# Search for the best pairs of the first two tiles divided into five parts at steps of their own; the first tile's search begins at step 36 instead of 40

## What is computed

```python
def peer_ffn(xn, w_query, sub_keys, u, v):
    def one_block(xb):                                   # 128 tokens
        q = (xb @ w_query).reshape(BLOCK, PEER_HEADS, 2, PEER_HALF)
        s = jnp.einsum('thcd,hckd->thck', q, sub_keys)   # scores against 2 x 128 sub-keys, 8 heads
        s1, i1 = lax.top_k(s[:, :, 0], PEER_TOPK)        # 16 best of each half
        s2, i2 = lax.top_k(s[:, :, 1], PEER_TOPK)
        cand_s = (s1[..., :, None] + s2[..., None, :]).reshape(BLOCK, PEER_HEADS, 256)
        cand_i = (i1[..., :, None] * N_KEYS + i2[..., None, :]).reshape(BLOCK, PEER_HEADS, 256)
        top_s, top_c = lax.top_k(cand_s, PEER_TOPK)      # 16 best pairs
        expert = jnp.take_along_axis(cand_i, top_c, axis=-1)
        g = jax.nn.softmax(top_s.astype(jnp.float32), axis=-1)
        ue, ve = jnp.take(u, expert, axis=0), jnp.take(v, expert, axis=0)
        act = jax.nn.gelu(jnp.einsum('thkd,td->thk', ue, xb), approximate=False)
        return jnp.einsum('thk,thkd->td', g * act, ve)
```

## Time and profile before

| what | value |
|---|---|
| median of 3 runs | 1881.32 us (1880.59 to 1883.3) |
| the profiled execution's own time | 1884.28 us |
| its span | 1882.5 us |
| mean granted TensorE clock | 0.967 |
| busy, share of the span | PE 94%, PEld 79%, DVE 71%, ACT 38%, POOL 35% |
| steps 36 to 62 in the span | about 490 to 735 us |

### The profile page before, as it was taken

How to read it: one execution, slowest core, us unless ns; L and a number is a source line. 1 busy time by engine, 2 the same in 40 slices (tenths; PEclk the granted TensorE clock), 3 DMA queues, 4 the chain that set the end, 5 groups by cost and what they waited for, 6 DMA issues and landing times.

```text
span 1882.5 us, 24827 instructions
## 1 busy us (share of the span) xinstructions
PE 1778.0 (94%) x8763; PEld 1483.5 (79%) x8767; DVE 1344.6 (71%) x2706; ACT 721.2 (38%) x1201; POOL 660.8 (35%) x416
## 2 busy tenths in 40 slices
PE   5899998999878989999989998999899999999998
PEld 4788875554555678999989998999788888888886
DVE  6843268465546877979979953992588888888886
ACT  4333334141222232355435533553343343343342
POOL 3234320000000332677676777776322222222220
PEclk9899997999898999999989999999899999999999
DMA  3222202434242662588887899886999999899993
GB/s 126 68 84 95 91 30 105 158 110 152 96 155 90 206 201 84 163 294 282 281 325 261 286 360 406 309 284 208 362 361 334 327 333 333 328 333 332 328 333 118
DMA packets 170192, 429.78 MB, mean 228 GB/s; under 512 B 15328, under 2 KB 66144, under 8 KB 165744
## 3 DMA queue, kind: packets, MB, share of 16 engines
q1 hardware_dynamic: 133056, 294.23, 45.4%
q0 software_dynamic: 36864, 134.23, 19.3%
q10 hardware_dynamic: 176, 0.07, 0.0%
HBM read 384.44 MB, written 44.04 MB: 228 GB/s over the span
## 4 chain that ended last, share of the span: by engine, by line
PE 73%; DVE 6%; DMA 3%; ACT 1%; issue 1%; POOL 1%; DVEq 0%; ACTq 0%
PE psum L1864 28%; PE psum L1161 8%; PE psum L1162 8%; PE psum L1163 8%; PE psum L1103 6%; PE psum L1187 5%; PE psum L1090 3%; PE psum L1011 3%; DMA u<-in_u 2%; PE psum L1059 1%; POOL ul L1401 1%; PE psum L1142 1%; DMA act_mat<-act_w 1%; DVE nmax L1460 1%; DVE hits L1615 1%
## 5 line engine op out<-in xcount | busy, mean ns | idle before, releaser
L1401 POOL TENSOR_TENSOR ul<-u,uh 128x1024 fp32r<-128x1024 f32 x128 | 321.8, 2515 | 532.3 <-ACT uh L1319 531.0
L1161 PE MATMUL psum<-split,uh 128*128 128x384 f32 x1024 | 357.0, 349 | 13.8 <-POOL ul L1401 13.8
L1163 PE MATMUL psum<-split,ul 128*128 128x384 f32 x1024 | 345.1, 337 | 0.0
L1162 PE MATMUL psum<-split,uh 128*128 128x384 f32 x1024 | 345.1, 337 | 0.0
L1844 POOL DMA_INDIRECT v_row<-in_v,gv x128 | 122.3, 956 | 383.5 <-DVE psum L1922 369.9
L1864 PE MATMUL psum<-vl,wh 128*128 128x512 f32 x768 | 240.9, 395 | 0.0
L1161 PEld LDWEIGHTS psum<-split,uh 128*128 128x128 f32 x1024 | 194.6, 190 | 18.0 <-POOL ul L1401 16.3
L1162 PEld LDWEIGHTS psum<-split,uh 128*128 128x128 f32 x1024 | 194.6, 190 | 1.4 <-issue 1.4
L1163 PEld LDWEIGHTS psum<-split,ul 128*128 128x128 f32 x1024 | 194.1, 190 | 0.0
L1864 PEld LDWEIGHTS psum<-vl,wh 128*128 128x128 f32 x768 | 144.9, 189 | 33.9
L1922 DVE SCALAR_TENSOR_TENSOR psum<-v_row,w,psum 128x1024 f32<-128x1024 f32 x127 | 162.8, 1282 | 0.0
(11 more groups left out here) (291 smaller groups left out, 3376.0 us busy)
## 6 DMA issues: line engine op xcount, KB each, us to landing
u<-in_u SPq DMA_DIRECT2D x128, 512.0 KB, 5.0
v<-in_v SPq DMA_DIRECT2D x64, 1024.0 KB, 5.0
act_mat<-act_w SPq DMA_DIRECT2D x128, 192.0 KB, 5.1
act_v<-act_mat SPq DMA_DIRECT2D x64, 384.0 KB, 6.7
wraw<-in_w_wide SPq DMA_DIRECT2D x18, 1024.0 KB, 5.1
gate_mat<-stage SPq DMA_DIRECT2D x16, 1024.0 KB, 10.1
gate<-gate_mat SPq DMA_DIRECT2D x128, 128.0 KB, 6.1
w_low<-in_w_branch_b SPq DMA_DIRECT2D x8, 1024.0 KB, 5.2
```

Of the source, the lines that this page charges most:

```text
L1161: nc.tensor.matmul(out, high[:, c], split[:, 0:DENSE, 0, c], start=(c == 0), stop=False)
L1162: nc.tensor.matmul(out, high[:, c], split[:, 0:DENSE, 1, c], start=False, stop=False)
L1163: last = nc.tensor.matmul(out, low[:, c], split[:, 0:DENSE, 0, c], start=False, stop=(c == DC - 1))
L1401: nc.gpsimd.tensor_tensor(ul[:, n % U_COLS], u[:, n % U_COLS], uh[:, n % UH_COLS].bitcast(F32), ALU.subtract).then_inc(s["u_low"], 1)
```

## The change

`best` is cut into its five parts, `best(part)`, the last with the cast and the shift. The tables now give each part a step. For search 0 the `find` parts move from steps 40 to 44 to steps 36 to 40, `pair_up` from 45 to 41, and `best` from step 46 to steps 42 to 46; its picks stay. For search 1 `find` and `pair_up` stay; `best` goes from step 58 to steps 58, 58, 59, 59 and 60, and the four picks from steps 59, 60, 61, 62 to 61, 61, 62, 62. ScalarE's `exps(0)` stays at step 47, and `exps(1)` goes from step 59 to step 61. No instruction is added or taken away.

```diff
-FIND_AT = ((40, 41, 42, 43, 44), (52, 53, 54, 55, 56))
-PAIR_AT = (45, 57)
-BEST_AT = (46, 58)
-PICK_AT = ((48, 49, 50, 51), (59, 60, 61, 62))
+FIND_AT = ((36, 37, 38, 39, 40), (52, 53, 54, 55, 56))
+PAIR_AT = (41, 57)
+BEST_AT = ((42, 43, 44, 45, 46), (58, 58, 59, 59, 60))
+PICK_AT = ((48, 49, 50, 51), (61, 61, 62, 62))
...
-                if step == BEST_AT[0] + 1:
+                if step == BEST_AT[0][-1] + 1:
                     exps(0)
...
-            def best():
-                for part in range(5):
-                    link(search(part, top, top_at, cand, PEER_HEADS))
+            def best(part):
+                link(search(part, top, top_at, cand, PEER_HEADS))
+                if part < 4:
+                    return
                 link(nc.vector.tensor_copy(top_at_f[:], top_at[:]))
...
-                    if step == BEST_AT[r]:
-                        best()
-                    if step in PICK_AT[r]:
-                        pick_out(HIT_HEADS * PICK_AT[r].index(step))
+                    for part in range(5):
+                        if step == BEST_AT[r][part]:
+                            best(part)
+                    for k, at in enumerate(PICK_AT[r]):
+                        if step == at:
+                            pick_out(HIT_HEADS * k)
```

More of the change, by code:

```diff
@@ L1371, in _ @@
                     column(step - 1 - FIRST_COLUMN)
-                if step == BEST_AT[1] + 1:
+                if step == BEST_AT[1][-1] + 1:
                     exps(1)
@@ L1664, in chosen_beside @@
                 for r in range(2):
-                    if step in FIND_AT[r]:
-                        find(r, FIND_AT[r].index(step))
+                    for part in range(5):
+                        if step == FIND_AT[r][part]:
+                            find(r, part)
                     if step == PAIR_AT[r]:
                         pair_up()
-                    if step == BEST_AT[r]:
-                        best()
-                    if step in PICK_AT[r]:
-                        pick_out(HIT_HEADS * PICK_AT[r].index(step))
+                    for part in range(5):
+                        if step == BEST_AT[r][part]:
+                            best(part)
+                    for k, at in enumerate(PICK_AT[r]):
+                        if step == at:
+                            pick_out(HIT_HEADS * k)
                     if step == SETTLE_AT[r]:
```

## The result

| what | before | changed |
|---|---|---|
| median of 6 runs each, the two side by side | 1880.95 us (1876.89 to 1883.74) | 1866.09 us (1857.45 to 1868.38) |
| ratio, 95% interval | 1 | 0.9908 (0.989 to 0.9925) |
| the profiled execution's own time | 1884.28 us | 1865.89 us |
| its span, mean granted TensorE clock | 1882.5 us, 0.967 | 1864.1 us, 0.974 |

The changed kernel is 0.9% faster by the ratio; the two medians lie 14.9 us (0.8%) apart, and the ratio is not their quotient. Between the two profiled executions lie 18.4 us, forecast 16.6.

The account below looks back on a forecast made before the run. TensorE, busy 94% of the span, was taken to wait mainly for VectorE, with low clock behind gaps. Terms −1.1 + 3.2 + 1.2 + 5.9 + 7.4 = 16.6 us gave 1867.7 us profiled, 1864.7 us median; range 1860.5 to 1871.

Parts of the forecast that it names:

- A: Steps 36 to 41: find parts placed earlier, one uncovered ahead of out_b, lose 1.1 us (bounds 0.9 to 2.1).
- B: Step 43: out_a comes earlier, its 2.18 us wait ends and value runs faster, a gain of 3.2 us.
- C: OUT_LEFT in step 43: starts from a busy stretch instead of a low clock, a gain of 1.2 us (0 to 3.0).
- D: Steps 46 to 51: refinement and row start earlier, fewer GpSimd holds, a gain of 5.9 us (1.8 to 6.4).
- E: Steps 58 to 60: waits for row and headT and the slow QUERY_LEFT go, gain 7.4 us (at least 5.8).
- the gap is shorter than any in rows 2 that had a low clock behind it: Steps 36 to 41: reason for taking a loss of 1.1 us, not 2.1 with value at low clock too.
- I take 1.2, near the second row: OUT_LEFT, step 43: chosen between 0 and 3.0 us, near the 1.4 from a similar product behind 3.60 us of idle.
- rival of the long gain: OUT_LEFT at full clock (+1.8) and no VectorE hold (+0.5): 18.9 us gained, 1862.4 us; chance 0.12.
- short gain: Bad VectorE holds, or OUT_LEFT and step 39's value at low clock: 1868.2 us, 1872 with nearly all; chance 0.18.
- a wait of 0.5 to 2 us for `out_b` in step 51: Step 51: sign that VectorE, with three picks ahead of out_b, sets the time; before, TensorE waited 0.16 us.
- rival of full DMA engines: Around 1130 us: DMA traffic ends independently of TensorE, so up to 16.6 us is returned, 1881 us; chance 0.07.
- rival that the clock turns the sign: Steps 36 to 45: added VectorE parts keep TensorE's clock at 0.50, three slow products cost 21 us, 1886 us; chance 0.03.

Follow-up runs that it names:

- three_parts_early: Changed kernel, search 0's find parts at steps 36, 37, 38, 42, 43, pair_up at 45, best whole at 46: 1875.53 us, ratio 0.996.
- same_again: The changed kernel unaltered, run once more: 1862.46 us, ratio 0.989 to the kernel before.
- search0_only: Changed kernel with search 1 put back at its old steps, so only search 0 is moved: 1873.17 us, ratio 0.9949.
- picks_only: Changed kernel with best of search 1 whole at step 58, its picks staying at 61, 61, 62, 62: 1867.14 us, ratio 0.9918.
- two_more_picks: Changed kernel with the last pick of search 1 made two more times in step 62: 1864.49 us, ratio 0.9907.
- four_more_picks: Changed kernel with the last pick of search 1 made four more times in step 62: 1875.44 us, ratio 0.9961.
- best_whole_at_46: Changed kernel with best of search 0 left whole at step 46: 1869.48 us, ratio 0.9932.
- search1_only: Changed kernel with search 0 put back at its old steps 40 to 46, so only search 1 is moved: 1873.99 us, ratio 0.9955.
- part_behind_out_b: Changed kernel with search 0's third find part moved behind out_b to step 39 and the fourth to 40: 1864.72 us, ratio 0.9891.
- part_behind_again: The kernel of part_behind_out_b run once more: 1860.96 us, ratio 0.9885.

## Why the prediction was right, and where its terms were not

| term | forecast | measured, changed kernel |
|---|---|---|
| A, steps 36 to 41 | -1.1 (-0.9 to -2.1) | -4.1 |
| B, `out_a` in step 43 | +3.2 | +3.4 |
| C, `OUT_LEFT` | +1.2 (0 to 3.0) | +2.9 |
| D, steps 46 to 51 | +5.9 (1.8 to 6.4) | +6.2 |
| E, steps 58 to 60 | +7.4 (5.8 or more) | +7.8 |
| sum | 16.6 | 16.2 |

**A was mis-sized, and outside its bounds.** The step "TensorE starts near 527.65 for 526.57" held: the wait is 0.99 us. What failed is the reason given for its clock, "the gap is shorter than any in rows 2 that had a low clock behind it". The gap was read alone; it lies between one of 2.17 us and one of 2.60, which were there before. The bound of 2.1 failed with it, since it allowed the low clock for `value` of step 39 only. In the changed kernel `value` of step 40 takes 1.89 us for 1.47 and `BRANCH_B` 8.83 for 7.13; with the slower turns of `out_b` and of the scores between them this makes the other 3 us. How often this happens, over the eight profiles in which the third part stands in front of `out_b` and the copies are as before:

| wait for out_b | profiles | 38 to 42 | BRANCH_B | OUT_LEFT |
|---|---|---|---|---|
| 0.92, 0.97, 0.99 | three_parts_early, same_again, changed | 42.6 to 42.7 | 8.83 | 8.83, 7.13, 7.13 |
| 0.67 to 0.90 | search0_only, picks_only, two_more_picks, four_more_picks, best_whole_at_46 | 39.4 to 39.8 | 7.13 | 7.13 |
| none | before, search1_only, part_behind_out_b, part_behind_again | 38.5 to 38.6 | 7.13 | 10.04 to 10.14 |

Five of eight came out near the forecast (0.9 to 1.3 us lost), three at 4.1. The order by the length of the wait is clean in these profiles, but the two groups are only 0.02 us apart. The length isn't the cause either: in all eight the wait ends 6.13 or 6.14 us after the turn of `row` in step 38 began, so VectorE's part is equally late, and only TensorE's arrival differs. It differs by where the low clock behind the gap of 2.17 us ended. The first four matmuls of the next scores, in the changed kernel and in search0_only:

```profile
524.20 1.67 PE L1011 MATMUL psum<-akT,abqT 128*128 128x512 f32 x4
```

```profile
523.83 2.15 PE L1011 MATMUL psum<-akT,abqT 128*128 128x512 f32 x4
```

In the four profiles with a wait of 0.67 or 0.68 us these four took 2.15 or 2.16 us, in the four with 0.90 to 0.99 they took 1.67 to 1.75; the second is also the picture in the four profiles without the wait (1.65 to 1.74), where `BRANCH_B` was never slow. So with the early return of the clock `BRANCH_B` was slow in three of four profiles with the wait and in none of four without it, and with the late return in none of four. What makes the clock return early or late in the same code, and why `BRANCH_B` was fast in best_whole_at_46 (wait of 0.90 us) and slow in three_parts_early (0.92), stays open.

**B** held to 0.2 us: the wait of 2.18 us is gone, and `value` takes 1.36 us for 2.35, as worked out.

**C** came out at its upper end: the step "I take 1.2, near the second row" priced `OUT_LEFT` from a product behind another gap. And its reason, that the engine comes from a busy stretch, is not the cause: that stretch is as busy in part_behind_out_b, where `OUT_LEFT` takes 10.05 us. C is coupled to A: without the wait in step 39 `OUT_LEFT` was slow, with it it was fast in seven of eight, and `BRANCH_B` was slow in three. What makes the one follow from the other is not shown. A and C taken as one sum to -1.2 here, +1.7 in the five profiles with the shorter wait, and 0 with the part behind `out_b`; the forecast had +0.1. The total came out right in part by luck: A was 3.0 us worse than forecast, C 1.7 better. The rival of the long gain had its mechanism in C (`OUT_LEFT` at full clock), that of the short gain in A.

**D** held in both its halves. The idle before the turn of `row` is 0.92 us (forecast 1), and the turn starts 5.1 us earlier relative to step 42 once B and C are taken off. The root set the time: VectorE idled 0.56 us for it. The holds by GpSimd came to 2.2 us (forecast 2.5, before 3.3). The sign "a wait of 0.5 to 2 us for `out_b` in step 51" was missed narrowly: the wait is 0.37 us, so VectorE only just set the time there. The timeline of VectorE after the change, steps 47 and 49:

```profile
597.12 0.16 DVE L196 RECIPROCAL inv_r<-root_r 128x1 f32<-128x1 f32 x1 [0.56 <-ACT root_r L1295]
...
615.35 2.02 DVE L1616 TENSOR_TENSOR hits<-top_at_f,iota 128x1600 f32<-128x1600 f32 x1
617.40 3.86 DVE L1619 TENSOR_TENSOR hits<-hits,code 128x1600 f32<-128x1600 f32 x1
621.30 1.82 DVE L1620 TENSOR_REDUCE pick<-hits 128x32 f32<-128x1600 f32 x1
```

One product of a pick took 3.86 us and another 2.02 for 1.82; the reduction beside them was not held. The Trainium skill (page "SBUF — State Buffer", section "SBUF: two separate sides") calls the shared ports an exclusive lock that is held for the whole instruction, so each of the three GpSimd operations could have cost one whole hold. The trace agrees with that as an upper bound: one of the three held a VectorE product by 2.04 us, another by 0.2, and the third met the reduction. Whether a second would do so was a matter of how they meet, as the range had it.

**E** held, and with it the two sub-forecasts. The root came 1.27 us after VectorE was free for it (forecast 1.1), and VectorE waited 1.50 for the turn (forecast 2.1). `QUERY_LEFT` takes 7.03 us. The prediction passed over why the two waits were there. In the kernel before, the cast at the end of `best`, 0.23 us in step 46, took ten times as long in step 58, while a `ul` of GpSimd ran from 692.03 to 694.43:

```profile
692.24 2.27 DVE L1609 CAST top_at_f<-top_at 128x128 f32<-128x128 uint32 x1
```

Without these 2.04 us `row` would have been some 2 us earlier and its wait of 2.18 us nearly nothing (an estimate by difference). The pick behind it was held in the same way, 4.00 us for 1.82. The cast took 2.27 and 2.28 us in picks_only and search0_only, whose waits are 2.17, and 0.32 in the changed kernel, where it stands behind `headT`. So what the division of `best` took away ahead of step 59 was a hold as much as an amount of work, and no run here tells the two apart.

**Nothing was given back.** In the stretches 860 to 1000, 1000 to 1200 and 1200 to 1345 us TensorE waited 6.7, 6.2 and 6.8 us in all, for 6.7, 7.1 and 6.7 before. The rival of full DMA engines falls: the traffic moves with TensorE. The rival that the clock turns the sign had its mechanism in A, in one product of four and not three. VectorE's slack before search 2 is 2.80 us, forecast 2.8, with two small errors that cancel: the copy came 7.8 us earlier (forecast 7.4), and VectorE was done 2.8 us later (3.2). One number of the prediction is off by itself: the short gain "with nearly all" of its terms is 1871 us by its own prices, as in the range, and not 1872.

## What to carry to other kernels

Work that an engine does for later is best placed by what stands directly behind it on that engine: here four to eight microseconds of search in front of `row`, `headT` or `out_a` cost TensorE between 2 and 6 us each, and cost nothing in front of something that is waited for anyway. Before taking such a move for final, read which engine the remaining waits name; the better gain here (another 9 to 11 us by the ratios) lay in letting ScalarE's copies go ahead of its exponentials, and it made the one remaining badly placed part visible, whose wait grew from 1.0 to 4.3 us. Price a gap on TensorE with the gaps around it, and give the slow products behind neighbouring gaps one common range instead of one each. Where two engines hold each other up, look for the instruction that takes several times its usual length before putting a wait down to the amount of work.

## What the runs showed of the hardware

A wait of 0.67 to 0.99 us on TensorE, between gaps of 2.17 and 2.60 us, went together with the clock of a product some 40 us later: `OUT_LEFT` took 10.04 to 10.14 us in four of four profiles without it, and 7.13 in seven of the eight with it (8.83 in the eighth, where another wait of 1.11 us had been put in front). `BRANCH_B`, 30 us ahead of `OUT_LEFT`, was slow in three of these eight (8.83 us for 7.13) and in none of the four. In the profiles of this case a product of 16 matmuls took 7.03 to 7.13 us, 8.37 to 8.83, or 10.04 to 10.14. The granted clock was 0.50 inside those of the longer ones that were looked at (8.83 and 10.05 us). So the price of this wait was 0.9 to 1.3 us in five profiles and 4.1 in three, with the same code up to that place, and the profile of a single execution does not tell which is the usual one.

While a GpSimd operation ran, a VectorE product of 1600 columns took up to 4.01 us for 1.82, and a cast of 128 columns 2.27 for 0.23. A reduction over 1600 columns kept its 1.82 us beside one.
